# Feed-forward tiles in three parts with a down product behind each, the up tile's row scale moved behind the product, and the low half of the inner tile on GpSimd

## The reference, cut to what matters

```python
hn = rms_norm(h, norm2_g)
gate, up = jnp.split(hn @ w_gate_up, 2, axis=-1)
h = h + (jax.nn.silu(gate) * up) @ w_down        # feed-forward 0
x = rms_norm(h, final_g)
...
def swiglu(h, w_gate, w_up, w_down):
    return (jax.nn.silu(h @ w_gate) * (h @ w_up)) @ w_down
x = x + 0.5 * swiglu(rms_norm_2(x, ffn1_norm[i]), ...)   # feed-forward 1
... # attention, gates, output projection
x = x + 0.5 * swiglu(rms_norm_2(x, ffn2_norm[i]), ...)   # feed-forward 2
x = x + jax.nn.sigmoid(rms_norm_2(x, ple_norm[i]) @ w_ple_gate[i]) * (p[i] @ w_ple_proj[i])
```

## Time and profile before

| | |
|---|---|
| median of 3 runs | 1999.79 us |
| profiled execution, first to last instruction | 1998.1 us |
| TensorE busy | 1990.9 us, 9505 matmuls |
| ScalarE busy | 732.3 us |
| VectorE busy | 877.9 us |
| GpSimd busy | 1007.5 us |
| granted TensorE clock, mean | 1.000 |

### The profile page before, as it was taken

How to read it: one execution, slowest core, us unless ns; L and a number is a source line. 1 busy time by engine, 2 the same in 40 slices (tenths; PEclk the granted TensorE clock), 3 DMA queues, 4 the chain that set the end, 5 groups by cost and what they waited for, 6 DMA issues and landing times.

```text
span 1998.1 us, 26696 instructions
## 1 busy us (share of the span) xinstructions
PE 1990.9 (100%) x9505; PEld 1668.7 (84%) x9505; DVE 877.9 (44%) x1467; ACT 732.3 (37%) x1034; POOL 1007.5 (50%) x795
## 2 busy tenths in 40 slices
PE   9999999999999999999999999999999999999999
PEld 8998887788888888888888888889888888888887
DVE  6587756535333322153334115677645523332124
ACT  6413234444222323232232225667643422322232
POOL 5444442245555544455555446565654555555443
PEclk9999999999999999999999999999999999999999
DMA  5233231133333332333332232332222333332332
GB/s 179 87 92 99 85 104 43 49 100 93 96 105 86 103 100 80 109 90 105 85 104 90 98 107 85 109 103 75 72 87 85 104 105 84 105 95 89 98 107 85
DMA packets 253787, 188.81 MB, mean 94 GB/s; under 512 B 6608, under 2 KB 249680, under 8 KB 253680
## 3 DMA queue, kind: packets, MB, share of 16 engines
q1 hardware_dynamic: 253024, 187.53, 31.5%
q10 hardware_dynamic: 688, 0.31, 0.1%
HBM read 180.93 MB, written 2.10 MB: 92 GB/s over the span
## 4 chain that ended last, share of the span: by engine, by line
PE 98%; ACT 1%; DVE 1%; issue 0%; DMA 0%; SPq 0%; ACTq 0%; DVEq 0%
PE ps L693 30%; PE ps L695 30%; PE ps L694 30%; PE ps L989 1%; PE ps L1141 1%; PE ps L1061 1%; PE ps L1062 1%; PE ps L1063 1%; PE ps L1129 1%; PE ps L1128 0%; PE ps L983 0%; PE ps L1111 0%; PE ps L1099 0%; PE ps L882 0%; PE ps L1098 0%
## 5 line engine op out<-in xcount | busy, mean ns | idle before, releaser
L566 POOL TENSOR_TENSOR wlo<-raw,whi 128x512 fp32r<-128x512 f32 (+2 forms) x636 | 852.9, 1373 | 862.1 <-ACT whi L1206 773.1
L693 PE MATMUL ps<-xh,whi 128*128 128x512 f32 (+1 forms) x1872 | 716.1, 383 | 0.0
L695 PE MATMUL ps<-xh,wlo 128*128 128x512 f32 (+1 forms) x1872 | 709.0, 379 | 0.0
L694 PE MATMUL ps<-xl,whi 128*128 128x512 f32 (+1 forms) x1872 | 708.7, 379 | 0.0
L1206 ACT ACTIVATE whi<-raw 128x2048 fp32r<-128x2048 f32 (+1 forms) x149 | 280.1, 1880 | 765.0 <-PE ps L695 764.9
L695 PEld LDWEIGHTS ps<-xh,wlo 128*128 128x128 f32 x1872 | 351.5, 188 | 66.8
L693 PEld LDWEIGHTS ps<-xh,whi 128*128 128x128 f32 x1872 | 351.7, 188 | 64.4 <-issue 0.7
L694 PEld LDWEIGHTS ps<-xl,whi 128*128 128x128 f32 x1872 | 352.0, 188 | 62.1 <-issue 0.7
L1736 DVE TENSOR_TENSOR tmp<-ps,rs 128x512 f32<-128x512 f32 x148 | 101.9, 691 | 313.1 <-PE ps L695 295.6
L695 PE MATMUL ps<-fh,wlo 128*128 128x512 f32 x528 | 205.4, 389 | 0.0
L693 PE MATMUL ps<-fh,whi 128*128 128x512 f32 x528 | 205.4, 389 | 0.0
(11 more groups left out here) (335 smaller groups left out, 2247.1 us busy)
## 6 DMA issues: line engine op xcount, KB each, us to landing
raw<-in_w_in SPq DMA_DIRECT2D x87, 512.0 KB, 4.6
raw<-in_w_gate_up SPq DMA_DIRECT2D x44, 512.0 KB, 4.7
raw<-in_ffn_w_gate SPq DMA_DIRECT2D x44, 512.0 KB, 4.0
raw<-in_ffn_w_up SPq DMA_DIRECT2D x44, 512.0 KB, 5.2
raw<-in_ffn_w_down SPq DMA_DIRECT2D x32, 512.0 KB, 4.0
raw<-in_w_down SPq DMA_DIRECT2D x16, 512.0 KB, 4.0
raw<-in_ffn_w_down SPq DMA_DIRECT2D x16, 384.0 KB, 3.6
raw<-in_w_b SPq DMA_DIRECT2D x8, 512.0 KB, 4.0
```

The costliest lines, as they stand in the source:

```text
L566: ins = pool.tensor_tensor(wlo[:, c % 2, cs], raw[:, c % 2, cs], whi[:, c % 2, cs].bitcast(F32), ALU.subtract)
L693: pe.matmul(o, w_of(whi), xhi, start=first, stop=False)
L694: pe.matmul(o, w_of(whi), xlo, start=False, stop=False)
L695: return pe.matmul(o, w_of(wlo), xhi, start=False, stop=last)
```

## The change

The feed-forward's 22 inner tiles are made in three parts of 7, 8 and 7 (`UPS`). Behind each part stands a down product of 4 chunks that takes 6, 8 and 8 inner tiles (`DOWN_K`) and makes all eight output tiles; each is added to `hT` at once, so every output tile is updated three times. `fh` and `fl` become rings of 9 tiles. The number of chunks and of their columns stays the same; loops over chunks are written out on all engines.

The up result isn't scaled: the product is silu(scaled gate) times the raw up result, read from PSUM, and the row scale is applied to the down result instead, in two operations where there was one (a multiply by factor and row scale from PSUM into `tmp`, then an add onto `hT`). The low half `fl` is made by GpSimd (`act_low`): behind the low half of the next weights within a part, ahead of them at a part's end. On ScalarE the silu now stands ahead of the next chunk's high copy, and in a down chunk of the last part the high copy stands ahead of that chunk's two feeds. The scaling of `hT` in layer 1 moves to the first down chunk of the first part.

The diff also brings a whole path for "folded" up tiles, those with a number of `PLAIN` or more. `PLAIN = FK` (22), and up tiles are numbered 0 to 21, so `folded` is never true; `FORMS_AT` is empty. Some semaphores are merged, and the mixer's `tmp` is named `gt`, at its old place.

```diff
-DOWN_K = (8, 8, 6)
+DOWN_K = (6, 8, 8)
+UPS = (7, 8, 7)
+PLAIN = FK
+RING = 9
+FORMS_AT = {}
+FFN_LEN = FK + 12
+PLACES = [place for r in range(3)
+          for place in [("up", sum(UPS[:r]) + n) for n in range(UPS[r])] + [("down", r, j) for j in range(4)]]
+def folded(p):
+    return up_tile(p) is not None and up_tile(p) >= PLAIN
...
 # GpSimd
+            def act_low(f, p):
+                n = up_tile(p)
+                pool.wait_ge(h_hi, FK * f + n + 1)
+                pool.tensor_tensor(fl[:, n % RING, :], tmp[:, 3, :], fh[:, n % RING, :].bitcast(F32), ALU.subtract).then_inc(h_split, 1)
+            def ffn(f):
+                low(C_F[f])
+                low(C_F[f] + 1)
+                for p in range(1, FFN_LEN):
...
+                    if down_part(p) is not None and up_tile(p - 1) is not None:
+                        act_low(f, p - 1)
+                    if p + 1 < FFN_LEN:
+                        low(C_F[f] + p + 1)
+                    if down_part(p) is None and up_tile(p - 1) is not None:
+                        act_low(f, p - 1)
 # TensorE
+            def down_chunk(f, p):
+                c = C_F[f] + p
+                r, j = down_part(p)
+                k0 = sum(DOWN_K[:r])
+                pe.wait_ge(w_lo, c + 1)
+                for t in range(2):
+                    pe.wait_ge(acc_free, 2 * (c - 2) + t + 1)
+                    for k in range(DOWN_K[r]):
+                        if j == 0 and t == 0:
+                            pe.wait_ge(h_split, FK * f + k0 + k + 1)
+                        o, z = CW * k + P * t, (k0 + k) % RING
+                        mm = passes(ps[:, bank(c, t), :], c % 2, lambda wt: wt[:, c % 2, o:o + P],
+                                    fh[:, z, :], fl[:, z, :], k == 0, k == DOWN_K[r] - 1)
+                    mm.then_inc(tile_done, 1)
 # ScalarE
-                def up(c, n, per=0, i=None):
-                    high(c + 2, per, i)
-                    act.wait_ge(acc_free, lin(2 * c + 1, 2 * per, i))
-                    act.activation(tmp[:, 1, :], tmp[:, 0, :], ACT.Silu).then_inc(silu_done, 1)
-                    act.wait_ge(h_done, lin(FK * f + n + 1, per, i))
-                    act.activation(one(fh, lin(n, per, i)), tmp[:, 3, :], ACT.Copy).then_inc(h_hi, 1)
...
+                act.wait_ge(rt_done, S + 1)
+                for p in range(FFN_LEN):
+                    c, n = C_F[f] + p, up_tile(p - 1)
+                    def coming(z):
...
+                        elif p and z == 0:
+                            high(c + 1)
...
+                    if n is not None and not folded(p - 1):
+                        act.wait_ge(acc_free, 2 * (c - 1) + 1)
+                        act.activation(tmp[:, 1, :], tmp[:, 0, :], ACT.Silu).then_inc(silu_done, 1)
+                    coming(0)
...
+                    if n is not None:
+                        act.wait_ge(h_done, FK * f + n + 1)
+                        act.activation(fh[:, n % RING, :], tmp[:, 3, :], ACT.Copy).then_inc(h_hi, 1)
...
+                    if down_part(p) is not None and down_part(p)[0] == 2:
+                        for t in range(2):
+                            m = 2 * down_part(p)[1] + t
+                            act.wait_ge(h_new, 3 * DK * f + 2 * DK + m + 1)
+                            feed(S + 1, m, gain)
+                high(C_F[f] + FFN_LEN + 1)
 # VectorE
-                        scaled(tmp[:, 0, :], c + j, 0, 2, i)
-                        scaled(tmp[:, 2, :], c + j, 1, 2, i)
...
+                for p in range(FFN_LEN):
+                    c, n, last = C_F[f] + p, up_tile(p - 1), FK * f + (up_tile(p - 1) or 0)
...
+                    if n is not None:
+                        dve.wait_ge(silu_done, last + 1)
+                        if last:
+                            dve.wait_ge(h_split, last)
...
+                            done(c - 1, 1)
+                            link(dve.tensor_tensor(tmp[:, 3, :], tmp[:, 1, :], ps[:, bank(c - 1, 1), :], ALU.mult))
+                            dve.sem_inc(acc_free, 1)
+                            dve.sem_inc(h_done, 1)
...
+                    if up_tile(p) is not None:
+                        done(c, 0)
+                        dve.wait_ge(silu_done, FK * f + up_tile(p))
+                        dve.tensor_tensor(tmp[:, 0, :], ps[:, bank(c, 0), :], rsx, ALU.mult).then_inc(acc_free, 1)
+                        continue
+                    r, j = down_part(p)
+                    if f == 1 and (r, j) == (0, 0):
+                        for n in range(DK):
+                            x = hT[:, n, META:TM]
+                            stt(x, x, vec[:, V_FIN + n:V_FIN + n + 1], ssum[:, META:TM], ALU.mult, ALU.mult).then_inc(xn_done, 1)
+                        dve.wait_ge(xn_done, DK)
+                    if (r, j) == (2, 0):
+                        clear(S + 1)
...
+                    for t in range(2):
+                        m = 2 * j + t
+                        x = hT[:, m, META:TM]
+                        done(c, t)
...
+                        stt(tmp[:, 2, :], ps[:, bank(c, t), :], factor, rsx, ALU.mult, ALU.mult).then_inc(acc_free, 1)
+                        dve.wait_ge(acc_free, 2 * c + t + 1)
+                        dve.tensor_tensor(x, x, tmp[:, 2, :], ALU.add).then_inc(h_new, 1)
+                        if r == 2:
+                            dve.wait_ge(h_new, 3 * DK * f + 2 * DK + m + 1)
+                            feed(S + 1, m, gain)
```

More of the change, by code:

```diff
@@ L105, in seen_from, with up_tile, down_part, fold_no @@
     return max(P * j - META, 0)
+PLACES = [place for r in range(3)
+          for place in [("up", sum(UPS[:r]) + n) for n in range(UPS[r])] + [("down", r, j) for j in range(4)]]
+def up_tile(p):
+    return PLACES[p][1] if 0 <= p < FFN_LEN and PLACES[p][0] == "up" else None
+def down_part(p):
+    return PLACES[p][1:] if 0 <= p < FFN_LEN and PLACES[p][0] == "down" else None
+def folded(p):
+    return up_tile(p) is not None and up_tile(p) >= PLAIN
+def fold_no(f, p):
+    return (FK - PLAIN) * f + up_tile(p) - PLAIN
+def ffn_place(c):
+    return next(((f, c - C_F[f]) for f in range(3) if C_F[f] <= c < C_F[f] + FFN_LEN), (None, -1))
 def lin(value, per=0, i=None):
@@ L322, in n_cols @@
                 return DK * (P + KW)
-            for d in C_D:
-                if d <= c < d + 12 and (c - d) % 3 == 2:
-                    return DOWN_K[2] * CW
-            return CH
+            part = down_part(ffn_place(c)[1])
+            return CH if part is None else DOWN_K[part[0]] * CW
         def value_tile(c, t, z):
@@ L836, in ffn @@
                       steps=None if S == 2 else lambda t, k: norm_sums(S, c) if (t, k) == SUMS_AT else None)
[L837 to L857 removed]
+                for p in range(1, FFN_LEN):
+                    if folded(p):
+                        fold_chunk(f, p)
+                    elif up_tile(p) is not None:
+                        chunk(c + p, xh, xl)
+                    else:
+                        down_chunk(f, p)
             opening()
@@ new lines, in fold_forms @@
+            def fold_forms(f, i, gain):
+                for z, n in enumerate((i, i + 4)):
+                    ins = act.activation(ps[:, 1, FOLD * z:FOLD * z + FOLD], hT[:, n, META:META + FOLD], ACT.Copy,
+                                         scale=vec[:, gain + n:gain + n + 1])
+                ins.then_inc(fs_in, 1)
+                for z in range(2):
+                    act.wait_ge(fs_sum, 2 * (4 * f + i) + z + 1)
+                    act.activation(fsh[:, 2 * z:2 * z + 2, i, :], ps[:, 5 + 2 * z, :].rearrange("p (y t) -> p y t", y=2),
+                                   ACT.Copy).then_inc(fs_hi, 1)
@@ L1255, in ffn @@
+            def ffn(f, S, own, gain):
                 root(S)
@@ new lines, in corner_sums @@
+            def corner_sums(f, p, m):
+                c, n = C_F[f] + p, fold_no(f, p)
+                if n:
+                    dve.wait_ge(sum_lo, 3 * n - 2 + m)
+                if m == 0:
+                    dve.wait_ge(corner_in, n + 1)
+                    dve.tensor_tensor(sums(3), sums(1), corner(c, 0, 0), ALU.subtract).then_inc(corner_sum, 1)
+                elif m == 1:
+                    dve.wait_ge(corner_sum, 3 * n + 1)
+                    dve.tensor_tensor(sums(5), sums(3), corner(c, 1, 1), ALU.subtract).then_inc(corner_sum, 1)
+                else:
+                    dve.wait_ge(corner_sum, 3 * n + 2)
+                    dve.tensor_tensor(sums(7), sums(5), corner(c, 1, 0), ALU.add).then_inc(corner_sum, 1)
```

392 lines of the change are left out of this document (260 added, 132 removed).

## The result

The changed kernel takes 2009.91 us (median of four runs, 2009.58 to 2010.06) against 1999.82 for the kernel before, measured beside it (1999.69 to 2000.12): a ratio of 1.005 with a 95% interval of 1.0036 to 1.0064. It is slower by 10.1 us, where 13.3 were forecast.

The account below looks back on a forecast made before the run. TensorE was taken as full in all three layers, so any late weights show in full. Terms 3.0 + 0.1 + 1.8 + 4.6 + 0.45 + 1.7 + 1.7 = 13.3 us on 1999.8 gave 2013.1 us, range 2003 to 2019.

Parts of the forecast that it names:

- last parts of layers 1 and 2: Next weights' low half late at the last part's borders, by 0.5, 0.6 and 0.6 us: 1.7 us in each layer.
- a clock below 1.00: Granted TensorE clock in the profile after; named among the signs that the prediction was wrong.
- start of layer 0: Third chunk's low half, behind the first silu, ready at 508.7 where needed at 508.65: +0.1 us.
- start of layer 1, gap: Third chunk's high copy stands behind the first silu, which waits for the row scale: TensorE 3.0 us late.
- rival B: Gaps slow the clock, or written-out code comes late: 4 to 7 us in all, 2018; chance 0.14.
- scaling of `hT`: Layer 1's first down chunk: eight VectorE scalings take turns with GpSimd's five pieces, ready at 10.0 against 8.16: +1.8 us.
- last part of layer 0, three borders: Added add and a feed ahead of every high copy make next weights late by 1.2, 1.7 and 1.7: 4.6 us.
- norm's sums wait for `ssum2`: Behind layer 0's last part, the norm's sums wait for VectorE's `ssum2`: +0.45 us.
- The walk: Operation-by-operation timing of the last part's chunks from its start, giving 4.6 us in layer 0 and 1.7 in each other layer.
- written-out loops: Last projection chunks were already written out, at 0.2267 us per matmul, so writing out loops was put at 0 us.
- The turns at the port: VectorE operations with two SBUF inputs and GpSimd pieces exclude each other; each meeting costs GpSimd's pieces 0.45 us.
- rival A: Pieces and VectorE operations interleave without port turns, decided at the last part's second chunk: 2003.3, within 0.2%; chance 0.12.

## Why the prediction was right, and which terms were off

Direction, mechanism and the three places were right: a TensorE that had nothing to lose, and five waits, all released by `wlo`, where they were said to be. Two signs went against it: no gap of half a microsecond in the last parts of layers 1 and 2, and a clock of 0.999, where a clock below 1.00 had been named as a sign of being wrong. The sum was 13.3, the measured difference 10.1. Term by term, in the trace of after:

| term | forecast | measured |
|---|---|---|
| start of layer 0 | 0.1 | 0 |
| start of layer 1, gap | 3.0 | 2.61 |
| slow matmuls behind it (rival B) | 0 | 1.7 |
| scaling of `hT` | 1.8 | 1.47 |
| last part of layer 0, three borders | 4.6 | 3.27 |
| norm's sums wait for `ssum2` | 0.45 | 0 |
| last parts of layers 1 and 2 | 1.7 + 1.7 | 0.1 each |

- **Start of layer 1.** From the rs product on, the chain took 875.65 - 866.57 = 9.08 us where rows of before made it 9.46. Silu to high copy was 0.54 instead of 0.63, and the low half to TensorE 0.05 instead of 0.2.
- **Last parts.** The step that was mis-sized is the length of the hand-overs. The walk took 1.05 from `hT` to `xh` out of the earlier trace rows; in after it is 0.73 (814.42 to 815.15), as in the kernel before with its loops written out. The odd tile started at 11.08, not 11.3, behind the part's start at 802.62, and TensorE followed 0.05 behind the low half. These are 0.32 + 0.22 + 0.15 = 0.69 us at each border. Against it, in layer 0 the low half had three meetings to pay for, 6.38, where I counted two: 1.2 - 0.69 + 0.45 = 0.96, and 0.94 was measured. The same sum gives 1.46 for the second and the third border, where 1.00 and 1.01 were measured: the walk had VectorE free at 23.9 and the odd tile 1.8 late, while it started at 825.74, 23.1 behind the part's start and 1.0 late. In layers 1 and 2 there is no third meeting: 0.5 - 0.69 leaves it in time, and the rows show it: the low half ends at 1205.26, TensorE starts at 1205.37, when it was due, and loses 0.07 at its next start. So an error of half a microsecond on a chain that comes nine times was worth 4.5 us: the rows had the right number for the operations and a wrong one for the time between them, which is longer inside a loop, and the change wrote the loops out ("0 us" for the written-out loops was this mistake).
- **The add** is a part of it, with the feeds ahead of the high copy at every chunk: take away the add or change the order, and the term goes. The prediction named both and priced them together, which was right.
- **The turns at the port** held as forecast: 1.78 and 1.76 for the sums, 5.92 and 6.38 for the pieces, 8.97 for six scalings. The Trainium skill's rule (SBUF — State Buffer, Who interferes with whom) agrees with each of them, and with the adds that read PSUM, 0.69 at all 72 places; rival A is out. What the rule doesn't tell, and the run with the high copy between the feeds does, is whether a turn costs time. One bound was added up wrongly: with each later piece losing 0.69, the scaling's gap comes to 2.8, not 2.5; nothing else hangs on it.
- **`ssum2`.** The sums' matmuls start 0.43 us apart where others are 0.2267, but they do so in the kernel before as well; the wait I added was not there, since `ssum2` was ready at 854.02 and the matmuls that need it start at 855.81.
- **Rival B** was priced at 2.2 us a gap and given 0.14; the longest of the five gaps brought it, for 1.7 us, in both profiled executions of this kernel, and by the clock in eight of nine. It belonged in the sum, as an uncertain term at the longest gap, rather than in a case of its own.
- **Hidden, as said:** `fl` on GpSimd within the up parts, the 48 updates of the first two parts, the later product.

So the total was nearer than its terms, and that part is luck: 4.5 us too much for the last parts, 0.4, 0.3 and 0.45 in smaller ones, and 1.7 us of slow matmuls too little, with 0.5 us of the measured difference in no term.

## What to carry to other kernels

Where TensorE is full, read the slack of the chain that prepares its next operand, border by border, and ask of each moved instruction what it now stands in front of on its engine; here three reorderings (one restores the order of the kernel before, two stand in neither kernel) won back all of the 9 us with the same operations. Contention makes a late chain later but costs nothing on one that starts early enough, so move the start before shortening the pieces. And take hand-over times from code of the same form: from a loop they are up to 0.4 us too long for code that is written out.

## What the runs showed of the hardware

- A hand-over between VectorE and ScalarE is 0.71 to 0.73 us start to start in written-out code and 0.95 to 1.24 (mostly 1.03 to 1.10) with addresses from a loop's register, the producer taking 0.68 in both; the one back is 0.82 to 0.85 (once 1.21) against 0.99 to 1.06.
- GpSimd takes 5.03 us for four 128x512 pieces and 6.07 for eight of 128x256: a piece has a cost of its own of about a quarter of a microsecond. Each VectorE operation that takes its turn adds 0.45 us.
- VectorE's add takes 0.69 us at all 72 places when one input is in PSUM; with both inputs in SBUF it took up to 1.57 beside GpSimd's pieces.
- A gap of 2.03 us or more (start-to-start excess) may be followed by 7 to 13 matmuls at the 1.2 GHz level, beginning at once (875.65) or 1.5 us later (668.17), and costing 1.7 to 2.9 us. The same gap in another place or execution isn't, and none up to 1.95 us was.
- The first matmul behind a wait for `wlo` costs 0.11 us more than the next.
